# A hybrid trunk's sparse stage: half of the value products as products of halves, weights landing in three slots

## The reference, cut to what matters

```
ss = q . k_sel - slope * distance ;  ps = masked_softmax(ss) ;  o_slc = ps @ v_sel
sw = q . k_win - slope * distance ;  pw = masked_softmax(sw) ;  o_win = pw @ v_win
o  = g0 * o_cmp + g1 * o_slc + g2 * o_win ;  y = silu(z) * o ;  h = h + y @ w_out
```

## Time and profile before

| | us |
|---|---|
| median of the runs | 1225.71 |
| lowest, highest run | 1225.02, 1226.03 |
| the profiled execution's own time | 1226.44 |
| its span | 1224.6 |
| TensorE busy | 1216.5 (99% of the span) |
| DVE busy | 727.4 (59%) |
| ACT busy | 559.2 (46%) |
| POOL busy | 40.7 (3%) |
| granted clock of TensorE | 0.999 |

### The profile page before, as it was taken

One profiled execution on the slowest core, in us unless ns is written; L12 is line 12 of the kernel. 1 busy time (PEld: TensorE's weight loads), 2 busy tenths in 40 slices (PEclk: granted clock), 3 DMA queues, 4 the chain that ended last, 5 costly groups with the idle time before them and its releaser, 6 DMA issues.

```text
span 1224.6 us, 15999 instructions
## 1 busy us (share of the span) xinstructions
PE 1216.5 (99%) x6164; PEld 1024.0 (84%) x6164; DVE 727.4 (59%) x875; ACT 559.2 (46%) x726; POOL 40.7 (3%) x47
## 2 busy tenths in 40 slices
PE   9999999999999999999999999999999999999997
PEld 8888888888888888888888888888888787887876
DVE  6654564564564564564564566564556577676776
ACT  6743343343343343343343356334355566473463
POOL 0000000000000000000000010000000000000000
PEclk9999999999999999999999999999999999999999
DMA  9965565565565565555565585645543455544522
GB/s 312 382 207 177 173 199 177 172 200 176 172 199 177 172 200 177 171 199 178 172 199 178 173 265 190 223 162 193 186 154 121 138 154 168 183 150 145 165 69 104
DMA packets 130158, 223.82 MB, mean 183 GB/s; under 512 B 7248, under 2 KB 40544, under 8 KB 129728
## 3 DMA queue, kind: packets, MB, share of 16 engines
q1 hardware_dynamic: 128096, 215.90, 54.0%
q0 software_dynamic: 1728, 7.10, 1.7%
q10 hardware_dynamic: 288, 0.18, 0.0%
HBM read 221.06 MB, written 2.10 MB: 182 GB/s over the span
## 4 chain that ended last, share of the span: by engine, by line
PE 98%; issue 1%; DVE 0%; ACT 0%; POOLq 0%; POOL 0%; DVEq 0%
PE acc L1147 23%; PE acc L1122 15%; PE acc L1124 15%; PE acc L1123 15%; PE acc L1148 12%; PE side L1122 2%; PE side L1124 2%; PE side L1123 2%; PE side L1312 2%; PE side L1395 2%; PE acc L1178 1%; PE side L1383 1%; PE side L1337 1%; PE side L1222 1%; PE acc L1182 1%
## 5 line engine op out<-in xcount | busy, mean ns | idle before, releaser
L766 DVE TENSOR_TENSOR w_lo<-w_raw,w_hi 128x2048 fp32r<-128x2048 f32 x194 | 443.9, 2289 | 325.1 <-ACT w_hi L513 323.9
L513 ACT CAST w_hi<-w_raw 128x2048 fp32r<-128x2048 f32 x194 | 369.6, 1911 | 346.0 <-PE acc L1124 229.8
L1147 PE MATMUL acc<-hT,w_hi 128*128 128x512 f32 x1216 | 431.7, 399 | 0.0
L1148 PE MATMUL acc<-hT,w_lo 128*128 128x256 f32 x1216 | 340.2, 280 | 0.0
L1147 PEld LDWEIGHTS acc<-hT,w_hi 128*128 128x128 f32 x1216 | 228.2, 188 | 54.0 <-issue 0.6
L1148 PEld LDWEIGHTS acc<-hT,w_lo 128*128 128x128 f32 x1216 | 229.5, 189 | 0.7
L1122 PE MATMUL acc<-w_hi,hT 128*128 128x512 f32 x480 | 187.6, 391 | 0.0
L1124 PE MATMUL acc<-w_hi,hT 128*128 128x512 f32 x480 | 187.0, 390 | 0.0
L1123 PE MATMUL acc<-w_lo,hT 128*128 128x512 f32 x480 | 186.8, 389 | 0.0
L1122 PE MATMUL acc<-w_hi,yT_hi 128*128 128x512 f32 x320 | 125.6, 393 | 0.0
L1124 PE MATMUL acc<-w_hi,yT_lo 128*128 128x512 f32 x320 | 124.6, 389 | 0.0
(11 more groups left out here) (204 smaller groups left out, 960.0 us busy)
## 6 DMA issues: line engine op xcount, KB each, us to landing
w_raw<-in_ret_w_in SPq DMA_DIRECT2D x180, 512.0 KB, 4.4
w_raw<-in_nsa_w_in SPq DMA_DIRECT2D x112, 512.0 KB, 4.5
w_raw<-in_ret_w_out SPq DMA_DIRECT2D x64, 512.0 KB, 4.6
w_raw<-in_nsa_w_out SPq DMA_DIRECT2D x32, 512.0 KB, 4.8
w_raw<-in_ret_w_in SPq DMA_DIRECT2D x23, 256.0 KB, 4.6
res<-in_x SPq DMA_DIRECT2D x2, 1024.0 KB, 10.8
arena<-in_nsa_cmp_w_k POOLq DMA_DIRECT2D x1, 2048.0 KB, 11.0
arena<-in_nsa_cmp_w_v POOLq DMA_DIRECT2D x1, 2048.0 KB, 10.8
```

The costliest lines, as they stand in the source:

```text
L513: act.copy(w_hi[:, s, :, :], w_raw[:, s, :, :]).then_inc(hi_done, 1)
L766: dve.tensor_tensor(w_lo[:, s, :, :], w_raw[:, s, :, :], w_hi[:, s, :, :].bitcast(F32), ALU.subtract).then_inc(lo_done, 1)
L1147: pe.matmul(parts[m][:, :], w_hi[:, s, i, w], hT[:, k, :, :], start=(k == 0), stop=False)
L1148: ins = pe.matmul(parts[m][:, 0:S], w_lo[:, s, i, w], hT[:, k, 0, :], start=False, stop=(k == KT - 1))
```

## The change

The 4 products of token tile 1 are made of halves, 3 single-pass products for each. For that ACT writes tiles 1 and 2 of a head rounded (`pT_hi`), DVE adds the rests (`pT_lo`, function `low_pT`, with the new semaphore `pT_low`), ACT rounds the group's V (`high_v`), and POOL makes its rest (`v_lo_now`). Token tile 0 stays a product of fp32 operands and reads V in place. `pT_lo` lies where the fourth slot of `w_raw` was: in the sparse stage chunks land in three slots (`LANDING = 3`), so a load waits for the `w_lo` of the chunk three before. `w_hi` and `w_lo` keep four slots. `low_pT` of a head is placed on DVE in the iteration of the chunk after the one behind which it was transposed, ahead of that iteration's w_lo; TensorE waits for it before the next head's transposes, and for that of the group's last head within the values, behind the two products of token tile 0.

```diff
+        LANDING = 3
+            fourth_landing.enter_context(nc.sbuf_tensor("first_three", [P, LANDING, KPC, COLS], F32))
+            pT_lo = fourth_landing.enter_context(nc.sbuf_tensor("pT_lo", [P, 2, 2, COLS], F32R))
...
+        def landing(g, c):
+            m = c if known(g, 0) else c - RING
+            return m % LANDING, 32 * (SPARSE_Q + m // LANDING + 1) + (0 if known(g, 0) else 32 * RING * g)
...
+            def chunk_of_three(g, c, w, k0, col):
+                l = landing(g, c)[0]
+                sp.wait_ge(lo_done, 4 * nsa_q(g) + c - LANDING + 1)
+                for to, src in by_rows(l, w, k0, col):
+                    sp.dma_start(to, src).then_inc(raw_in[l], 16)
...
-            def group_values(g):
-                if not known(g, 0):
-                    pool.wait_ge(pv_psum, g)
+            for g in range(G):
+                pool.wait_ge(v_now_hi, g + 1)
                 for b, v in enumerate((vs, vw)):
-                    ins = pool.tensor_copy(v_now[:, 2 * b:2 * b + 2, :], v[:, :, bass.ds(g * DH, DH)])
+                    ins = pool.tensor_tensor(v_lo_now[:, 2 * b:2 * b + 2, :], v[:, :, g * DH:(g + 1) * DH], v_hi_now[:, 2 * b:2 * b + 2, :].bitcast(F32), ALU.subtract)
                 ins.then_inc(v_now_ready, 1)
...
             def take_pT(g, r):
                 act.wait_ge(pT_psum, R * g + r + 1)
                 for b in range(2):
-                    act.copy(pT[:, b, :, r * P:(r + 1) * P], side[b][:, 0:3 * P].rearrange("p (a b) -> p a b", a=3))
+                    act.copy(pT[:, b, r * P:(r + 1) * P], side[b][:, 0:P])
+                    act.copy(pT_hi[:, b, :, r * P:(r + 1) * P], side[b][:, P:3 * P].rearrange("p (a b) -> p a b", a=2))
                 act.copy(pTc[0:64 + 3 * NC, r * P:(r + 1) * P], side[1][0:64 + 3 * NC, 3 * P:4 * P]).then_inc(pT_ready, 1)
+            def high_v(g):
+                if known(g, 0):
+                    act.wait_ge(v_taken, 2)
+                else:
+                    act.wait_ge(pv_psum, g)
+                for b, v in enumerate((vs, vw)):
+                    ins = act.copy(v_hi_now[:, 2 * b:2 * b + 2, :], v[:, :, g * DH:(g + 1) * DH])
+                ins.then_inc(v_now_hi, 1)
...
+                    if c == 1:
+                        high_v(g)
...
+            def low_pT(g, r):
+                dve.wait_ge(pT_ready, R * g + r + 1)
+                for b in range(2):
+                    ins = dve.tensor_tensor(pT_lo[:, b, :, r * P:(r + 1) * P], side[b][:, P:3 * P].rearrange("p (a b) -> p a b", a=2),
+                                            pT_hi[:, b, :, r * P:(r + 1) * P].bitcast(F32), ALU.subtract)
+                ins.then_inc(pT_low, 1)
...
                     if scored:
                         head_scores(*scored)
+                    if c - 1 in PROBS_AFTER[g]:
+                        low_pT(g, PROBS_AFTER[g].index(c - 1))
                     if taken:
...
                     pe.wait_ge(pT_ready, u)
+                    pe.wait_ge(pT_low, u)
...
             def weighted_values(g):
                 pe.wait_ge(pT_ready, R * g + R)
+                pe.wait_ge(score_read, R * g + R)
+                for b, v in enumerate((vs, vw)):
+                    pe.matmul(side[2][:, :], v[:, 0, g * DH:(g + 1) * DH], pT[:, b, :], start=(b == 0), stop=False)
                 pe.wait_ge(v_now_ready, g + 1)
-                pe.wait_ge(score_read, R * g + R)
-                for t, tiles in enumerate((((0, 0),), ((1, 0), (2, 1)))):
-                    first = True
-                    for b in range(2):
-                        for tile, keys in tiles:
-                            pe.matmul(side[2 + t][:, :], v_now[:, 2 * b + keys, :], pT[:, b, tile, :], start=first, stop=False)
-                            first = False
+                pe.wait_ge(pT_low, R * g + R)
+                for b in range(2):
+                    for keys in range(2):
+                        at, p_hi, p_lo = 2 * b + keys, pT_hi[:, b, keys, :], pT_lo[:, b, keys, :]
+                        pe.matmul(side[3][:, :], v_hi_now[:, at, :], p_hi, start=(at == 0), stop=False)
+                        pe.matmul(side[3][:, :], v_lo_now[:, at, :], p_hi, start=False, stop=False)
+                        pe.matmul(side[3][:, :], v_hi_now[:, at, :], p_lo, start=False, stop=False)
```

More of the change, by code:

```diff
@@ L84, in sem @@
             return ctx.enter_context(nc.semaphore(name))
+        LANDING = 3
+        with ExitStack() as fourth_landing:
+            fourth_landing.enter_context(nc.sbuf_tensor("first_three", [P, LANDING, KPC, COLS], F32))
+            pT_lo = fourth_landing.enter_context(nc.sbuf_tensor("pT_lo", [P, 2, 2, COLS], F32R))
         w_raw = sb("w_raw", [P, RING, KPC, COLS])
@@ L146, in aside @@
                 return sparse_part.enter_context(nc.sbuf_tensor(name, shape, dt))
-            aside("pT_place", [P, 2 * 3 * R * P])
+            aside("pT_place", [P, 2 * R * P])
+            pT_hi = aside("pT_hi", [P, 2, 2, R * P], F32R)
             pTc = aside("pTc", [P, R * P], F32R)
             cmp_prob_place = aside("cmp_prob_place", [P, 112], F32R)
-            aside("window_place", [P, 7040 - 3584 - 112])
+            v_lo_now = aside("v_lo_now", [P, 4, P], F32R)
+            aside("window_place", [P, 7040 - 4208])
+            with ExitStack() as late:
+                late.enter_context(nc.sbuf_tensor("late_place", [P, 6256 + 2 * SCORES - 7040], F32))
+                v_hi_now = late.enter_context(nc.sbuf_tensor("v_hi_now", [P, 4, P], F32R))
             vc_parts = aside("vc_parts", [P, G, 112], F32R)
@@ L176, in trunk @@
         both = vw_row[:, KT * NG + DH + G * NC:KT * NG + DH + 2 * G * NC]
-        pT = piece(0, 2, 3, R * P)
-        silu_zT = piece(4096, R, S)
+        pT = piece(0, 2, R * P)
+        silu_zT = piece(4208, R, S)
         y32 = silu_zT
-        qhT = piece(5120, R, S)
-        prob = piece(6144, 2, SCORES)
-        v_now = piece(6144 + 2 * SCORES, 4, P)
+        qhT = piece(5232, R, S)
+        prob = piece(6256, 2, SCORES)
         gatesT = arena[0:64 + NG, 0:S]
@@ L236, in trunk @@
         recip_done, factor_done, prob_ready = sem("recip_done"), sem("factor_done"), sem("prob_ready")
-        pT_psum, pT_ready, v_now_ready, pv_psum = sem("pT_psum"), sem("pT_ready"), sem("v_now_ready"), sem("pv_psum")
+        pT_psum, pT_ready, pT_low, v_now_hi, v_now_ready, pv_psum = sem("pT_psum"), sem("pT_ready"), sem("pT_low"), sem("v_now_hi"), sem("v_now_ready"), sem("pv_psum")
         zT_ready = sem("zT_ready")
@@ L272, in trunk @@
         NSA_TAIL_Q = nsa_q(G - 1) + 2
+        SPARSE_Q = nsa_q(0)
+        def landing(g, c):
+            m = c if known(g, 0) else c - RING
+            return m % LANDING, 32 * (SPARSE_Q + m // LANDING + 1) + (0 if known(g, 0) else 32 * RING * g)
         def nsa_chunks(g):
@@ L435, in _ @@
             sparse(G - 1)
-            outputs(NSA_TAIL_Q, nsa_out, G - 1)
+            for j in range(CG):
+                chunk_of_three(G - 1, 2 * RING + j, nsa_out, (G - 1) * KPC, j * COLS)
             for t in range(TT):
@@ L517, in ahead, with sparse_high @@
                 high(q + (c + 3) // RING, (c + 3) % RING)
+            def sparse_high(g, c):
+                l, landed = landing(g, c)
+                act.wait_ge(raw_in[l], landed)
+                act.wait_ge(chunk_done, 4 * nsa_q(g) + c - RING + 1)
+                act.copy(w_hi[:, c % RING, :, :], w_raw[:, l, :, :]).then_inc(hi_done, 1)
             def norm_high(j):
@@ L654, in _ @@
             for c in range(4 * KV_GROUPS):
-                ahead(KV_Q, c)
+                if c + 3 < 4 * KV_GROUPS:
+                    ahead(KV_Q, c)
+                else:
+                    sparse_high(0, c + 3 - 4 * KV_GROUPS)
                 if c == 0:
@@ L726, in sparse @@
                     else:
-                        ahead(q, c)
+                        sparse_high(g, c + 3)
                     if scored_before(g, c):
@@ L740, in _ @@
                 sparse(g)
-            ahead(NSA_TAIL_Q, 0)
+            sparse_high(G - 1, 2 * RING + 3)
             def final_scale(t):
@@ L769, in ahead, with sparse_low @@
                 low(q + (c + 3) // RING, (c + 3) % RING)
+            def sparse_low(g, c):
+                dve.wait_ge(hi_done, 4 * nsa_q(g) + c + 1)
+                dve.tensor_tensor(w_lo[:, c % RING, :, :], w_raw[:, landing(g, c)[0], :, :], w_hi[:, c % RING, :, :].bitcast(F32), ALU.subtract).then_inc(lo_done, 1)
+            def low_pT(g, r):
[4 more added lines that the diff above has]
+                ins.then_inc(pT_low, 1)
             def norm_low(j):
@@ L976, in _ @@
                     head_scores(0, 0)
-                ahead(KV_Q, c)
+                if c + 3 < 4 * KV_GROUPS:
+                    ahead(KV_Q, c)
+                else:
+                    sparse_low(0, c + 3 - 4 * KV_GROUPS)
                 if c == 0:
@@ L1052, in sparse @@
                     else:
-                        ahead(q, c)
+                        sparse_low(g, c + 3)
```

(2 more changed lines are left out.)

14 lines of the change are left out of this document (5 added, 9 removed).

## The result

The changed kernel takes 1228.54 us (median of 15 runs, 1227.25 to 1229.15) against 1226.03 us for the kernel before on the same chips (15 runs, 1225.01 to 1226.64): +2.5 us, a ratio of 1.002, 95% interval 1.0013 to 1.0027. The forecast was 1227.2 us, +1.46. The time lies in the range; the sign was right, and 1.0 us of loss was not in the sum. The interval leaves out 1, so the loss is real, if small.

A forecast was written before the change was run, and what follows sets the result against it. TensorE's own instruction stream, busy 99% of the span, was taken as the bound. Products -2.85, head 15 +0.68, stalls +2.10 and +1.33, restarts +0.20 gave +1.46 on 1225.71: 1227.2 us, range 1223.5 to 1229.2.

The forecast's parts named there:

- Term 1: TensorE's value products: 12 single-pass products replace 8 fp32 records, gaining 0.71 us a group, 2.85 us in four groups.
- Term 2: ACT's split copies from PSUM add 0.1 us a head; POOL's two subtractions are hidden by more than 20 us.
- Term 3: DVE's added low_pT delays what follows by 0.68 us; TensorE waits longer at three places, groups 0 and 3 are covered.
- head 15's transposes: Group 3: low_pT of head 14 joins DVE's unbroken chain ahead of TensorE's transposes, costing 0.68 us.
- values of group 1, the wait: TensorE asks for pT_low at 1037.93, DVE releases it at 1040.03: stall 2.10 us, plus 0.1 at the restart.
- values of group 2: TensorE asks for pT_low at 1113.57, released at 1114.90: stall 1.33 us, plus 0.1 at the restart.
- values of groups 0 and 3: low_pT is done before TensorE asks for it, so no stall in these two groups.
- Term 4: Weight loads wait for the w_lo three chunks before instead of four: spare 3.6 us at the tightest, cost 0.
- the rival of the clock: TensorE's clock falls in the new stall; each 2 us at the lower level costs 1 us, 1228.2 or more; chance 0.03.
- The forecast's own case: Stalls of 2.1 and 1.3 us in groups 1 and 2, sum within 1224.5 to 1228.1 us; chance 0.60.
- only the gain: Semaphores arrive in time in groups 1 and 2: 1223.5 us if only head 15 costs, else 1222.9; chance 0.14.
- the vector work costs in full: Each low_pT on DVE takes 1.15 us instead of 0.68 to pass: 1228.6, up to 1229.2 us; chance 0.19.

The follow-up runs named there:

- g1_early: Changed kernel with low_pT of group 1's last head one iteration earlier, ahead of chunk 8's w_lo: 1224.78 us, ratio 0.9992 to the kernel before.
- g2_early: Changed kernel with low_pT of group 2's last head ahead of the w_lo in chunk 7's iteration: 1226.27 us, ratio 1.0005 to the kernel before.
- the combined kernels: Changed kernel with early low_pT in groups 1 and 2 and one group 3 w_lo later: 1223.06 us; with group 3's last low_pT also earlier: 1222.62 us.
- landing_three: Kernel before with the three landing slots alone; values, copies and V as before: 1225.84 us, ratio 1.0001.
- all_four: Changed kernel with low_pT of the last heads of groups 1, 2 and 3 earlier and one group 3 w_lo later: 1222.62 us, ratio 0.9973.
- g3_swap: Changed kernel with one w_lo of group 3, in chunk 5's iteration, moved behind head 15's probabilities: 1227.97 us, ratio 1.0013 to the kernel before.
- stall_two: Kernel before with TensorE waiting, within group 1's values, for two small DVE additions behind the residual additions: 1229.79 us, ratio 1.003.
- stall_long: Kernel before with TensorE waiting, within group 1's values, for the w_lo behind the residual additions: 1231.43 us, ratio 1.0046.
- stall_short: Kernel before with TensorE waiting, within group 1's values, for the residual additions of chunk 8: 1227.46 us, ratio 1.0016.
- g1_mid: Changed kernel with low_pT of group 1's last head behind chunk 8's w_lo, ahead of its residual additions: 1225.84 us, ratio 1.0002 to the kernel before.

## Why the prediction was right, and where it was off

**Term 1 (products), mechanism right, 10% too large.** Each fp32 product was two records 0.43 us apart and went as reckoned. The products of halves come every (969.51 - 967.19) / 10 = 0.232 us, not 0.227, so a group gains 0.64 instead of 0.71: 2.6 us in all instead of 2.85. The measured cadence was the better guide than four passes for one, and even it was a little generous. The Trainium skill's four passes (FP8 and Floating Point Precision, TensorE Precision Notes) are 3.7 here, 0.858 by 0.232.

**Term 2 (ACT and POOL), right.** The copies of one branch now start 0.15 and 0.27 us apart, 0.42 together for 0.37, as the timeline of ACT in the changed kernel shows. POOL's subtractions take 1.15 and 0.74 us on the mean and nobody waits for them.

```profile
1032.48 0.27 ACT L724 COPY arena<-side 128x128 f32<-128x128 f32 x1
1032.63 0.38 ACT L725 CAST pT_hi<-side 128x256 fp32r<-128x256 f32 x1
1032.90 0.28 ACT L724 COPY arena<-side 128x128 f32<-128x128 f32 x1
```

**Term 3 (DVE's work and the late semaphores), right at all five places.** Timeline of DVE in groups 1 and 2, which answers to the earlier trace rows: low_pT stands behind the residual additions and behind the scaling, where the rows of before had put it, and lets the next operation start 0.66 us later (0.68 reckoned).

```profile
1036.81 1.29 DVE L853 TENSOR_TENSOR res<-acc,res 128x512 f32<-128x512 f32 x2
1038.01 0.75 DVE L814 TENSOR_TENSOR pT_lo<-side,pT_hi 128x256 fp32r<-128x256 f32 x2
1038.67 2.29 DVE L809 TENSOR_TENSOR w_lo<-w_raw,w_hi 128x2048 fp32r<-128x2048 f32 x1
...
1114.28 1.22 DVE L873 SCALAR_TENSOR_TENSOR arena<-arena,stage 128x1024 f32<-128x1024 f32 x1
1115.42 0.75 DVE L814 TENSOR_TENSOR pT_lo<-side,pT_hi 128x256 fp32r<-128x256 f32 x2
```

| place | reckoned (with restart) | in the trace |
|---|---|---|
| head 15's transposes | 0.68 | 1.07 - 0.41 = 0.66 |
| values of group 1, the wait | 2.20 | from 1034.99 + 1.72 = 1036.71 to 1038.90, and 0.08 at the restart: 2.27 |
| values of group 2 | 1.43 | 0.81 + 0.64 = 1.45 |
| values of groups 0 and 3 | 0 | 0 |

That these are causes and not only coincidences of the trace is shown by g1_early, g2_early and the combined kernels: taking the lateness away, with all of the work left in, gives the time back.

**Term 4 (landing slots), right.** landing_three is the kernel before with a ratio of 1.0001.

**The step that failed: the rival of the clock, with its chance of 0.03.** I had one place where the clock fell, the kernel's end, and took from it that over 4 us of idle time are needed. One fall read from one place says that this much is enough there; it doesn't say that less is safe. Nor could that trace show it: TensorE idles for 8.1 us in it, 6.9 of them at the end, so there was no pause of 2 us elsewhere. In the changed kernel 2.0 us were enough in 13 of 15 runs, by their times and clocks, and in its trace the fall cost 1.5 us. The mechanism and the price per microsecond stood in the text (0.45 instead of 0.23 us a product, measured 0.43); the chance was far too small, and the sum had nothing for it. The stalls that I had forecast set it off. The Trainium skill (TensorE: Matmul & The Clock Gate, Part 1) has the rule that an idle TensorE is throttled; I had set it aside for a pause of this length. The runs agree with the rule in that the clock fell to 0.50 with an idle stretch of 2.03 us before it; the page counts so short a pause as harmless, and there the measurement differs and decides. The two runs of the changed kernel in which the clock held best, 1227.25 and 1227.79 us, enclose the 1227.5 us that the forecast's +1.46 gives on the 1226.03 measured beside it.

**That the time fell in the range was in part luck.** The forecast's own case went up to 1228.1 us and its word "same" up to 1228.2; the median is 1228.54. The range reached that far only for another rival, costlier vector work, which the rows refute. By the table above the steps cost 3.33 us where the sum had 1.46: the clock 1.54 us, the smaller gain of the products 0.3 and the waits 0.1; stretches outside the steps of the table came out 1.1 us shorter in the profiled execution and hid a part of it.

The other rivals: "only the gain" fell with the two waits; "the vector work costs in full" fell with the 0.66 us of low_pT, though its time (1228.6) is the one that was measured, by another mechanism. A time that fits a rival does not show it; the rows do.

What stays open: why an idle time of 2.0 us at the same place lowers the clock in some executions of a program and not in others, and whether 13 of 15 runs of one kernel against 4 of 11 of another is a difference of the kernels. The counts are small, and the changed kernel was measured at another time than its variants. Not tested either is the kernel before with its own w_lo of group 3 moved: head 15's old wait of 0.4 us, which is in the 3.2 us that all_four gains, might be had without the products of halves.

## What to carry to other kernels

When work is split into smaller pieces that need one more operand, place the step that makes this operand by when its reader asks for it, not by where the loop has room: here the shorter products were worth 2.6 us and lost 4.4 us to late semaphores and 1.5 us to the clock they set off, while the same work in an earlier slot of the same engine left 1222.62 us, 0.27% below the kernel before. On an engine that is the bound, count an idle stretch at more than its length: it may also lower that engine's clock for a while after. And when a wait is taken away, look at the next semaphore on the way, which was late all along behind it.

## What the runs showed of the hardware that was not expected

- An idle stretch of TensorE of 2.0 us in a run that is otherwise busy was followed by a granted clock of 0.50 in some executions and of 1.00 in others (0.50 in the traces of the changed kernel and g3_swap, 1.00 in those of g2_early and stall_two). By the runs' times and clocks the clock fell in 13 of 15, 6 of 11, 4 of 11 and 3 of 5 runs of four kernels (the changed one, g3_swap, g2_early, stall_two). After 3.5 us it was 4 of 5 (stall_long); after 1.3 us none of 10 (stall_short), and after 0.85 us none of 10 (g1_mid).
- The fall is not tied to the restart: it came 1.1 us after TensorE had started again in the changed kernel (1038.90 to 1040), 0.6 us after in g3_swap and 0.6 us before in stall_long. It stayed at 0.50 for over 3 us each time, so the products that paid were those behind the idle stretch: 0.43 us apart instead of 0.23. The price was 1.5 us in the traces of the changed kernel and stall_long, and between the two groups of a kernel's runs 1.1 us (changed kernel), 1.4 (g3_swap), 1.5 (g2_early) and 2.1 (stall_two). In stall_long the four runs lie 2.0 to 3.7 us above the fifth; whether the clock fell more than once in the longest is not shown.
- A product of fp32 operands with 512 columns costs 0.858 us and one of halves 0.232 here, a ratio of 3.7.
